# A two-layer hybrid decoder on one core: norms refined in PSUM, a semaphore of its own for the last head's score pieces, and a new order of the steps

## The reference

```python
for l in range(DEPTH):
    h = rmsnorm(x, attn_norm[l])
    proj = jnp.einsum('bsd,de->bse', h, w_in[l])
    sb_q, sb_k, sb_v, sw_q, sw_k, sw_v = jnp.split(proj, splits, axis=-1)
    sb_o = stick_breaking_attention(...)               # 8 heads, strictly causal
    sw_o = sliding_window_sink_attention(...)          # 8 query heads on 2 kv heads, window 128, rope
    mix = concat(rmsnorm(sb_o, sb_norm[l]), rmsnorm(sw_o, swa_norm[l]))
    x = x + mix @ w_out[l]
    h = rmsnorm(x, mlp_norm[l])
    x = x + jnp.square(jax.nn.relu(h @ w_up[l])) @ w_down[l]
return rmsnorm(x, final_norm)
```

## Time and profile before

| | us |
|---|---|
| median of 3 runs | 1188.58 |
| lowest, highest | 1187.75, 1190.56 |
| the profiled execution, its own time | 1187.64 |
| its span | 1185.9 |
| PE busy | 1154.5 |
| ACT busy | 589.4 |
| POOL busy | 574.3 |
| DVE busy | 554.3 |

### The profile page before, as it was taken

The page is one execution under the profiler, slowest core; times in us unless marked ns, Lnnn a source line. Parts: engine busy times, 40 slices in busy tenths (PEclk is TensorE's granted clock), DMA queues, the critical chain, the costliest instruction groups (busy, mean ns, idle before and its releaser), DMA issues.

```text
span 1185.9 us, 15498 instructions
## 1 busy us (share of the span) xinstructions
PE 1154.5 (97%) x5546; PEld 968.4 (82%) x5546; DVE 554.3 (47%) x785; ACT 589.4 (50%) x940; POOL 574.3 (48%) x310
## 2 busy tenths in 40 slices
PE   7999998999999999999999999899999999999996
PEld 5788887878888888888888889687888888888886
DVE  7766678765222222223355666758532222222224
ACT  5789898544133233133346888965431422322442
POOL 3454754664444444444754564456454444444452
PEclk9999999999999999999999999999999999999999
DMA  5220211223322323222222121012233232232222
GB/s 188 72 71 19 90 36 36 91 87 99 99 94 100 107 88 105 90 89 96 99 72 72 54 69 50 25 54 90 89 107 107 89 103 93 88 106 88 97 81 72
DMA packets 30027, 99.65 MB, mean 84 GB/s; under 512 B 3600, under 2 KB 5648, under 8 KB 29968
## 3 DMA queue, kind: packets, MB, share of 16 engines
q1 hardware_dynamic: 28992, 97.80, 25.1%
q10 hardware_dynamic: 976, 1.08, 0.3%
HBM read 96.77 MB, written 2.10 MB: 83 GB/s over the span
## 4 chain that ended last, share of the span: by engine, by line
PE 88%; ACT 4%; DVE 3%; issue 1%; DVEq 1%; ACTq 1%; DMA 1%; SPq 0%
PE DW L441 24%; PE DW L443 24%; PE DW L442 24%; PE Z L441 2%; PE Z L443 2%; PE Z L442 2%; PE Z L594 2%; PE DW L528 2%; PE O L607 1%; PE Z L577 1%; PE O L552 1%; PE DW L524 1%; ACTq L813 1%; DMA raw<-in_weights 1%; PE DW L538 1%
## 5 line engine op out<-in xcount | busy, mean ns | idle before, releaser
L951 POOL TENSOR_TENSOR w<-raw,w 128x1024 fp32r<-128x1024 f32 x178 | 429.8, 2416 | 409.4 <-ACT w L701 405.5
L701 ACT ACTIVATE w<-raw 128x1024 fp32r<-128x1024 f32 x177 | 185.8, 1051 | 224.0 <-PE DW L443 212.4
L441 PE MATMUL DW<-xm,w 128*128 128x512 f32 x512 | 200.3, 391 | 1.6 <-issue 1.6
L441 PE MATMUL DW<-stage,w 128*128 128x512 f32 x512 | 199.5, 390 | 0.6 <-DVE stage L1256 0.6
L442 PE MATMUL DW<-xm,w 128*128 128x512 f32 x512 | 199.3, 389 | 0.0
L443 PE MATMUL DW<-xm,w 128*128 128x512 f32 x512 | 199.3, 389 | 0.0
L443 PE MATMUL DW<-stage,w 128*128 128x512 f32 x512 | 199.3, 389 | 0.0
L442 PE MATMUL DW<-stage,w 128*128 128x512 f32 x512 | 199.3, 389 | 0.0
L1281 DVE TENSOR_TENSOR kf<-o 128x512 f32<-128x512 f32 x64 | 58.1, 908 | 195.7 <-ACT o L886 195.5
L1297 DVE TENSOR_TENSOR DW<-DW,probs 128x512 f32<-128x512 f32 x62 | 43.4, 699 | 224.1 <-PE DW L443 224.1
L441 PE MATMUL DW<-xa,w 128*128 128x512 f32 x296 | 119.6, 404 | 9.5 <-DVE xa L1064 7.5
(11 more groups left out here) (226 smaller groups left out, 1681.3 us busy)
## 6 DMA issues: line engine op xcount, KB each, us to landing
raw<-in_weights SPq DMA_DIRECT2D x179, 512.0 KB, 3.3
x<-in_x SPq DMA_DIRECT2D x6, 256.0 KB, 5.6
out_x<-x SPq DMA_DIRECT2D x6, 256.0 KB, 2.5
raw<-in_weights SPq DMA_DIRECT2D x2, 256.0 KB, 4.2
x<-in_x ACTq DMA_DIRECT2D x2, 256.0 KB, 4.9
out_x<-x ACTq DMA_DIRECT2D x2, 256.0 KB, 2.5
work<-in_positions SPq DMA_DIRECT2D x1, 256.0 KB, 6.7
gains<-in_gains ACTq DMA_DIRECT2D x1, 28.0 KB, 3.6
```

What stands on the lines that cost most here:

```text
L441: pe.matmul(bank, w[:, slot, 0, k], rhs[:, 0, c], start=start, stop=False)
L701: act.activation(w[:, slot_of(l * PACKS + p), 0], raw[:, p % 2], ACT.Identity).then_inc(w_hi, 1)
L951: pool.tensor_tensor(w[:, slot, 1], raw[:, p % 2], w[:, slot, 0].bitcast(F32), ALU.subtract).then_inc(w_ready, 1)
```

## The change

Five edits and a new order:

1. The mean of a norm and the two middle results of its refinement lie in the PSUM bank `W[:, 0]`, where the sum of squares already is, and no longer in SBUF (attention, stick-breaking and MLP norm). The bank is released after the last step of the refinement, not after the mean. The sliding-window norm and the closing norm stay as they are.
2. Score pieces of the last head signal `zl_full`, those of the others `z_full`, so that pieces of head 7 may stand ahead of piece 13.
3. The square of the last pair of heads is made by ACT, from `o` into the bank `O`; DVE adds it from there. DVE signals ACT (`o_joined`) and waits for it (`o_squared`).
4. POOL waits for DVE's first sums (`start_summed`) ahead of its first CL step.
5. Both lists of steps are new; BS14 stands ahead of BS13.

```diff
-T0 U0 AG0 T1 CH3 U1 NP0 NA0 NAE0 NAD0 NAF0 TE0 T2 CL3 AG1 TH0 CH4 AG2 CL4 AG3 T3 U2 U3 AG4 AG5 TL0 CH5 TE2 AG6
+T0 U0 T1 U1 NP0 AG0 CH3 NA0 NAE0 NAD0 CL3 T2 NAF0 TE1 CH4 TE0 U2 AG1 TH1 AG2 AG3 AG4 T3 TH0 CL4 U3 CH5 AG5 TL0
...
-                        mm.then_inc(z_full, 1)
+                        mm.then_inc(zl_full if h == LAST_HEAD else z_full, 1)
...
-                        act.wait_ge(z_full, l * PIECES + n + 1)
+                        if h == LAST_HEAD:
+                            act.wait_ge(zl_full, l * 2 + n % 2 + 1)
+                        else:
+                            act.wait_ge(z_full, l * Z_PIECES + n + 1)
...
+                    elif step == "BD" and n == LAST_HEAD:
+                        act.wait_ge(o_joined, l + 1)
+                        act.activation(O[:, :], o[:, n // 2 % 2], ACT.Square).then_inc(o_squared, 1)
...
             pool.drain()
+            pool.wait_ge(start_summed, 2)
             for l, plan in enumerate(PLANS):
...
-                dve.tensor_scalar(mean, sums, -1.0 / width, EPS, ALU.mult, ALU.add).then_inc(w_drained, 1)
-
-            def norm_refine(count, mean, guess, dst):
+                return dve.tensor_scalar(mean, sums, -1.0 / width, EPS, ALU.mult, ALU.add)
+
+            def norm_refine(count, mean, guess, dst, last=None):
...
-                dve.scalar_tensor_tensor(dst, dst, 1.5, guess, ALU.add, ALU.mult)
-                dve.drain()
+                dve.scalar_tensor_tensor(dst if last is None else last, dst, 1.5, guess, ALU.add, ALU.mult)
+
+            def refine_in_psum(count, dst):
+
+                norm_refine(count, W[:, 0, :], work1, W[:, 0, :], dst)
+                dve.drain().then_inc(w_drained, 1)
...
-                        if n % 2:
+                        if n == LAST_HEAD:
+                            dve.drain().then_inc(o_joined, 1)
+                            dve.wait_ge(o_squared, l + 1)
+                            dve.tensor_tensor(acc[:, 1], acc[:, 1], O[:, :], ALU.add)
+                            dve.drain().then_inc(sb_o, 1)
+                        elif n % 2:
```

More of the change, by code:

```diff
@@ L134 @@
-WD7 U17 BH11 BL11 BX10 SQ7 GH0 XE10 BA4 TE17 GL0 SA6 SA7 NW0 XH10 BO4 BS12 NWE0 BD4 NWD0 NWF0 BE12 MN0 BX11
-MN1 XL10 XE11 BS13 BP12 XH11 BE13 MN2 BP13 BH12 XL11 MH0 VT17 BL12 BH13 VH17 BA5 MN3 MH1 MH2 ML0 ML1 BL13 BX12
-GH1 MH3 VL17 BS14 BX13 XE12 XH12 ML2 XE13 BS15 BE14 BO5 ML3 BP14 XL12 BE15 XH13 OS0 CL20 BD5 OS1 BP15 BH14
-BH15 XL13 GH2 GL1 CH21 BL14 OS2 OS3 BA6 OE0 BX14 BL15 CH22 OE1 XE14 OE2 GL2 BX15 XE15 XH14 CL21 BO6 CL22 OE3
-CH23 OS4 OE4 XH15 BD6 XL14 OS5 XL15 OE5 CH24 BA7 OS6 CL23 BO7 BD7 CL24 OS7 GH3 OE6 OE7 GL3 NS0 NSE0 NSD0 NSF0
+T0 U0 T1 U1 NP0 AG0 CH3 NA0 NAE0 NAD0 CL3 T2 NAF0 TE1 CH4 TE0 U2 AG1 TH1 AG2 AG3 AG4 T3 TH0 CL4 U3 CH5 AG5 TL0
@@ new lines @@
+SA3 BH8 WS6 WA5 WM6 T15 U14 WE6 BP9 BL8 WO5 BH9 WR6 XL7 U15 WN6 WT6 TE14 CH17 TH14 BL9 WD5 WH6 BX8 CL17 XE8
+BA3 TL14 TE15 BO3 BX9 BS10 WL6 WS7 CH18 SA4 XE9 WM7 BS11 VT15 BE10 CL18 BD3 T16 U16 WE7 WR7 VH15 WN7 WA6 XH8
+BP10 CH19 BE11 CL19 WT7 XL8 VL15 SQ5 T17 TE16 WO6 WH7 CH20 WD6 WL7 BH10 BP11 WA7 SA5 XH9 U17 BL10 TH16 SQ6 WO7
+WD7 TL16 TE17 BX10 SQ7 XL9 BH11 GH0 SA6 XE10 BA4 BL11 GL0 SA7 XH10 NW0 BO4 BS12 BX11 NWE0 BE12 NWD0 VT17 NWF0
+XL10 XE11 BS14 BS13 MN0 XH11 MN1 BE13 BP12 MH0 MH1 BD4 MN2 MH2 XL11 BP13 ML0 MN3 BA5 VH17 BH12 ML1 BS15 BO5
@@ L153 @@
-CL19 WE7 BE10 TE15 VT15 BD3 WR7 XE9 XH9 WN7 SA4 U16 SQ5 SA5 BP10 WA6 VH15 VL15 WT7 XL8 WO6 XL9 BS11 BH10 WD6
-WH7 SQ6 WL7 T17 WA7 TE16 VT16 CH20 BE11 BL10 BP11 U17 SA6 WO7 VH16 WD7 BH11 SQ7 BL11 SA7 GH0 TE17 TH17 VL16
-TL17 BX10 NW0 XE10 BS12 NWE0 BE12 NWD0 NWF0 BA4 MN0 BX11 MN1 XH10 BO4 XE11 MN2 BS13 BP12 BS14 MN3 MH0 BH12
-BE13 CL20 BL12 ML0 BS15 BX12 GL0 XH11 XL10 BP13 MH1 MH2 BD4 XL11 BH13 BL13 BA5 ML1 MH3 ML2 ML3 BE14 BP14 XE12
-BX13 XE13 BH14 XH12 OS0 BO5 OS1 BL14 OE0 XL12 BE15 BD5 BX14 BP15 XH13 XL13 OS2 GH1 BH15 XE14 BA6 BL15 CH21
@@ new lines @@
+TE16 BP11 SA5 U17 SQ6 VT16 XL9 BX10 WO7 BH11 WD7 TE17 CH20 SQ7 SA6 BL11 GH0 VH16 SA7 VL16 TH17 NW0 XE10 TL17
+BS12 NWE0 NWD0 NWF0 MN0 MN1 BA4 MN2 BE12 XH10 BX11 BP12 XE11 BS14 BS13 MH0 BO4 BH12 ML0 BE13 CL20 BL12 XH11 GH1 MH1
+XL10 GL0 MN3 BP13 BD4 BH13 MH2 BS15 MH3 BL13 ML1 BE14 BX12 XL11 ML2 BA5 ML3 BP14 BO5 BX13 XE12 XE13 BH14
+XH12 OS0 BD5 OS1 BE15 OS2 BL14 BP15 GH2 OE0 OS3 BH15 XL12 BL15 BX14 OE1 CH21 CH22 CL21 GL1 XH13 OE2 XE14 BX15
+XE15 XL13 OE3 CH23 BA6 GL2 XH14 BO6 XH15 BD6 XL14 OS4 OS5 XL15 BA7 BO7 BD7 CL22 OS6 OE4 OE5 OS7 GH3 GL3 CH24
@@ L160 @@
+OE6 NS0 OE7 NSE0 CL23 CL24 NSD0 NSF0
 """
```

86 lines of the change are left out of this document (44 added, 42 removed).

## The result

| | before | after |
|---|---|---|
| median, 20 runs each | 1189.01 us | 1191.22 us |
| fastest and slowest of them | 1187.75 and 1191.62 | 1190.34 and 1192.08 |
| profiled execution, span | 1185.9 | 1189.5 |

The ratio is 1.0016, 95% interval 1.001 to 1.0022. The changed kernel is slower, by about 2 us, and its time lies above the predicted range (1182.5 to 1189.0). Note the second row: the kernel before is spread over 3.9 us, the changed one over 1.7 us at the upper end of that; the last part of "The prediction, point by point" says why.

A forecast was written before the change was run, and what follows sets the result against it. TensorE bounds it, busy 1154.5 of 1185.9 us. From 1187.64: start -0.9, PSUM norms -1.6, last head's swap +0.56 (layer 0) and -0.1 (layer 1), middles -0.4 and -0.9, plus 0.94 to the median: 1185.2 us; range 1182.5 to 1189.0.

The follow-up runs named there:

- x7: The changed kernel with GpSimd's split of the first MLP weight block cut to a quarter of its columns in each layer; 1191.39 us, 1.0017 of before.

## What to carry to other kernels

An operation made shorter on an engine that shares a port with GpSimd only helps if the next two-SBUF operation doesn't run into the next GpSimd operation; look at when those start, measured from what sets them off, before counting the gain. In a reordering, ask of every gap that is left what stands right behind it: a gap ahead of a full stretch of matmuls costs the gap and, where the clock falls, up to half the time spent at half clock (1.4 us of 3.4 in x7), so the high half that releases the matmuls goes first on ACT. And take a clock stretch in one profile as one draw: compare the fastest, the median and the slowest of the timed runs, and their mean clocks, before a difference of 2 us in one profile is put down to the code.
